# Output projection of a hybrid decoder step: the sample tile from unsplit float32 weights in two column groups, placed ahead of the last transposes

## The chip, the cores and the metric

The kernel runs on one core of one Trainium2 chip. Its engines work side by side and wait for each other on semaphores: TensorE (PE in the profile, PEld for its weight loads), VectorE (DVE), ScalarE (ACT), GpSimd (POOL) and SyncE (SP, which here only issues DMAs). The metric is the device time of one execution in microseconds (us); less is better. All times below come from runs on the chip.

## The reference

One inference step of a decoder layer for a prompt (16 meta tokens and 1024 tokens) and a sample group (8 sequences of 8 new tokens, so 64 rows). The part that the change touches is the very last one:

```python
y = jnp.concatenate([o_gla * jax.nn.silu(gg),
                     o_pool.astype(dt) * jax.nn.silu(pg),
                     o_fox.reshape(B, T, FOX_W).astype(dt) * jax.nn.silu(fg)], axis=-1) @ wo
return h + rmsnorm(y, post)          # wo is 1024 x 1024, h the input rows
```

Everything is float32. The attention part (`fox`) gives 384 of the 1024 columns of `y`, in three pairs of heads; its last pair of heads is what the kernel works on just before the projection.

## The kernel before, in words

Stages in order: input projection (up to about 470 us of the trace), softmax attention of the prompt in 12 "quarters" (pair of heads p = 0..2, 256 query rows q = 0..3) with the sample group's attention over its cached pages woven in, and from about 594 us the output projection.

**What sets the order.** The function `plan()` writes one list of steps; every engine walks it and does its own part of each step. The letters that matter here: `S` is a user of one of two score slots in PSUM (two banks each, taken in turn): a block of scores (`P1`), a block of transposes (`T`, with its quarter and number), or a tile of the output projection (`proj`). `V` is the product of a transposed block of probabilities with the values. `R sum` brings the inverse row sums to the rows of the quarter. `W k` copies row block k (of 8) of the output weights, rounded to the fast matmul format fp32r, into `woh` (ACT, `wo_high`); `X k` makes the remainder, raw weights minus `woh`, into `wol` (DVE, `wo_low`). `Y t` does the same split of the rows of `y`, `yh` on ACT (`y_high`) and `yl` on POOL. `E t` finishes a tile: sums of squares on ACT (`squares_out`), scaling, residual and output on DVE (`finish`). The table `TAIL` hangs `W`, `X` and `Y` steps behind units of the last two quarters.

**A tile of the projection** (`project_out`, `product`) is 3 products in fp32r for each of 8 row blocks and 2 halves of 512 columns: `yh` with `woh`, `yh` with `wol`, `yl` with `woh`; 48 matmuls of 512 columns. Nine tiles: first the sample's 64 rows, then eight of 128 prompt rows. The stationary operand is `y`, so the sample's 64 rows take as many matmuls of 512 columns as 128 rows do.

**Memory.** `wol_a` (remainders of row blocks 0 to 5) lies exactly over `wo_raw_a`, the raw weights, and `wol_b` (6 and 7) over `wo_raw_b`: `wo_low` writes each remainder in place. The tile's two halves lie in the two banks of its slot, on the same partitions; the slot is free for a next user when `finish` has read both halves (its second instruction on L1610).

A matmul of plain float32 is two instructions on TensorE in the trace (the products on L2053 and L2010); one of fp32r is one; a transpose is one.

Of the kernel before, what the change touches and what calls it, by code (L numbers as in the profile page):

```python
# [150 lines left out]
def plan():  # L151
# [66 lines left out]
    for n, t in enumerate(PROJ):  # L218
        if n >= 2:
            order.append(("Y", ("proj", t)))  # L220
        if n:
            order.append(("E", ("proj", PROJ[n - 1])))
        order.append(("S", ("proj", t)))
# [18 lines left out]
def slot_of(user):  # L242
    return SF[user] % 2


P1S = [k for k in SUSERS if k[0] == "P1"]
# [8 lines left out]
def build(nc, a, o):  # L255
    with ExitStack() as ctx:
# [6 lines left out]

        YF = sb("YF", [P, 14 * NT])
# [44 lines left out]
        def stage(*tensors):  # L309
            with ExitStack() as s:  # L310
                return [s.enter_context(nc.sbuf_tensor(n, d, t)) for n, d, t in tensors]

# [10 lines left out]
        wol_a, _, yh0, yl0, yh1, yl1, xres, zout, woh, wol_b, gpost = stage(  # L323
            ("wol_a", [P, 6, D], F32R), ("pad_a", [P, 6 * NT - 6 * D], F32),
            ("yh0", [P, KT, P], F32R), ("yl0", [P, KT, P], F32R), ("yh1", [P, KT, P], F32R),
# [103 lines left out]
        out_half, half_squared = sem("out_half"), sem("half_squared")  # L429

# [64 lines left out]
        def s_emptied(eng, user):  # L495
            eng.wait_ge(s_free[slot_of(user)], PROJ.index(user[1]) // 2 + 1)
# [276 lines left out]
        def _(pool):  # L773
# [114 lines left out]
            for n_, t in enumerate(PROJ):  # L888
                g.wait_ge(yhi_done, n_ + 1)
                m = P if t < NTILE else NS  # L890
                g.tensor_tensor(yl[n_ % 2][:, :, 0:m], Y[:, :, ycol(t):ycol(t) + m], yh[n_ % 2][:, :, 0:m].bitcast(F32),  # L891
                                ALU.subtract).then_inc(ylo_done, 1)

        @block.scalar
        def _(act):
# [236 lines left out]
            def squares_out(user):  # L1132

                t = user[1]
                n_ = PROJ.index(t)
                m = P if t < NTILE else NS
                low, high = slice(0, D // 2), slice(D // 2, D)
                act.wait_ge(out_half, n_ + 1)
                if n_:
                    act.wait_ge(d_y, 32 * n_)  # L1140
                act.activation(zout[0:m, low], s_slot(user)[0:m, low], ACT.Square, accum_out=zhalf[0:m, 0:1]  # L1141
                               ).then_inc(half_squared, 1)
# [3 lines left out]
                act.activation(zout[0:m, high], s_slot(user)[0:m, high], ACT.Square, accum_out=zstat[0:m, 0:1]  # L1146
                               ).then_inc(half_squared, 1)
# [13 lines left out]
            def y_high(n_):  # L1161

                t = PROJ[n_]
                m = P if t < NTILE else NS
                if t < NTILE:
                    drained(act, ("sum", 2, t // 2))
                else:
                    drained(act, ("s_outT", NB - 1))
                if n_ >= 2:
                    s_ready(act, ("proj", PROJ[n_ - 2]))  # L1170
                act.activation(yh[n_ % 2][:, :, 0:m], Y[:, :, ycol(t):ycol(t) + m], ACT.Copy).then_inc(yhi_done, 1)  # L1171

            for kind, key in PLAN:
                if kind == "Y":
                    y_high(PROJ.index(key[1]))
# [30 lines left out]
        def _(dve):  # L1206
# [389 lines left out]
            def wo_low(k):  # L1596
                dve.wait_ge(wohi_done, k + 1)
                dve.tensor_tensor(wol[k], wo_raw[k], woh[:, k, :].bitcast(F32), ALU.subtract).then_inc(wolo_done, 1)  # L1598

            def finish(user):  # L1600
# [7 lines left out]
                for n_half, cols in enumerate(halves):  # L1608
                    dve.wait_ge(half_squared, 2 * n_ + n_half + 1)
                    ins = dve.tensor_tensor(zout[0:m, cols], s_slot(user)[0:m, cols], gpost[0:m, cols], ALU.mult)  # L1610
# [73 lines left out]
        def _(pe):  # L1684
# [385 lines left out]
            def project_out(user):  # L2070
                t = user[1]
                n_ = PROJ.index(t)
                m = P if t < NTILE else NS
                s_taken(pe, user)
                out = s_slot(user)
                pe.wait_ge(yhi_done, n_ + 1)
                pe.wait_ge(ylo_done, n_ + 1)
                pe.wait_ge(wolo_done, KT)
                for half in range(2):
                    cols = slice(512 * half, 512 * half + 512)  # L2080
                    ins = product(out[0:m, cols], lambda k: (yh[n_ % 2][:, k, 0:m], yl[n_ % 2][:, k, 0:m]),
# [56 lines left out]
```

## Time and profile before

| | |
|---|---|
| Median of 3 runs | 701.57 us (701.45 to 702.39) |
| The profiled execution | 700.78 us |
| Its span in the trace | 699.1 us |
| PE busy | 658.0 us, 94% of the span |
| DVE, ACT, POOL busy | 393.3, 262.1, 142.9 us |
| Output projection, first matmul to the end | 593.82 to 699.1 us |

The trace starts later and ends earlier than the execution: 1.68 us lie around its span. Times in rows are counted from the start of the span. Busy times of one engine cannot be added to those of another, since they overlap; on PE an instruction's own duration holds its passage through the array, so that in a dense stream one starts before the one ahead of it has ended.

### The profile page before, as it was taken

Reading aid. Unit: us, or ns where it says so; the run is one execution under the profiler, and the core shown is the slowest. Engines: PE = TensorE matmul, PEld = TensorE weight load, DVE = VectorE, ACT = ScalarE, POOL = GpSimd, SP = SyncE. Lnnn points to the kernel's source line nnn. Section 1 sums busy time; section 2 is a strip of 40 time slices with the busy share of each in tenths; the row PEclk is TensorE's granted clock in tenths of the full one; section 3 lists DMA queues with packets and bytes.
Section 4 is the critical chain, followed back from the end, with each engine's and each line's share of the span. In section 5 each row is a group of like instructions: output and inputs, shape, how many; then the busy total and the mean of one; then the engine's idle time right before and its main releaser. Section 6 shows DMA issues by size and latency. Waiting matters only on the chain.

```text
span 699.1 us, 13106 instructions
## 1 busy us (share of the span) xinstructions
PE 658.0 (94%) x5120; PEld 565.0 (81%) x5120; DVE 393.3 (56%) x706; ACT 262.1 (37%) x480; POOL 142.9 (20%) x162
## 2 busy tenths in 40 slices
PE   2999999999999999999999989989999997999996
PEld 2799999898999889999999955766576655688885
DVE  4824926672455305169999965444433559345543
ACT  6637344111111346122121155645574566231321
POOL 4034112111111011233312040222222103112210
PEclk9999999999999999999999999999999999999999
DMA  8411103131100032352210381667676512033232
GB/s 248 124 38 49 43 1 75 29 94 31 32 26 8 4 84 97 98 166 77 61 31 1 119 272 42 179 180 209 186 226 176 207 37 100 9 98 106 75 122 90
DMA packets 60759, 67.29 MB, mean 96 GB/s; under 512 B 15188, under 2 KB 50907, under 8 KB 60697
## 3 DMA queue, kind: packets, MB, share of 16 engines
q1 hardware_dynamic: 55529, 51.37, 24.9%
q0 software_dynamic: 5168, 15.08, 7.3%
q8 instruction: 41, 0.67, 0.4%
q14 instruction: 21, 0.17, 0.1%
HBM read 57.71 MB, written 8.68 MB: 95 GB/s over the span
## 4 chain that ended last, share of the span: by engine, by line
PE 82%; DVE 9%; ACT 4%; issue 2%; SPq 1%; DMA 1%; DVEq 0%
PE PS L1764 14%; PE PS L1765 13%; PE PS L1766 13%; PE PS L1693 5%; PE PS L1692 5%; PE PS L1694 5%; PE PS L2053 3%; PE PS L2035 3%; PE PS L1988 3%; PE PS L2010 2%; PE PS L1953 2%; PE PS L1940 2%; DVE rows_odd L1576 2%; DVE YF L1455 1%; DVE wol_a L1598 1%
## 5 line engine op out<-in xcount | busy, mean ns | idle before, releaser
L1764 PE MATMUL PS<-xh,wh 128*128 128x368 f32 x576 | 196.1, 340 | 0.3 <-DVE RA L1392 0.3
L1765 PE MATMUL PS<-xl,wh 128*128 128x368 f32 x576 | 190.2, 330 | 0.0
L1766 PE MATMUL PS<-xh,wl 128*128 128x368 f32 x576 | 189.8, 329 | 0.0
L582 POOL TENSOR_TENSOR wl<-wr,wh 128x1024 fp32r<-128x1024 f32 x24 | 61.5, 2560 | 292.0 <-ACT wh L944 291.7
L1764 PEld LDWEIGHTS PS<-xh,wh 128*128 128x128 f32 x576 | 108.2, 188 | 4.4 <-issue 1.8
L1765 PEld LDWEIGHTS PS<-xl,wh 128*128 128x128 f32 x576 | 108.2, 188 | 0.9
L1766 PEld LDWEIGHTS PS<-xh,wl 128*128 128x128 f32 x576 | 108.2, 188 | 0.0
L1264 DVE TENSOR_TENSOR wr<-wr,small 128x1024 f32<-128x1024 f32 (+1 forms) x26 | 37.1, 1426 | 43.3 <-DMA wr<-in_w_in_dram 43.2
L1692 PE MATMUL PS<-woh,yh 128*128 128x512 f32 (+1 forms) x144 | 56.1, 390 | 0.6 <-DVE wol_b L1598 0.6
L1435 DVE RECIPROCAL RA<-RA 128x1104 f32<-128x1104 f32 x8 | 56.4, 7053 | 0.3
L1694 PE MATMUL PS<-woh,yl 128*128 128x512 f32 (+1 forms) x144 | 56.0, 389 | 0.0
L891 POOL TENSOR_TENSOR yl<-YF,yh 128x1024 fp32r<-128x1024 f32 (+1 forms) x9 | 22.7, 2520 | 107.3 <-ACT yh L1171 107.3
L2010 PE MATMUL PS<-YF 64*128 64x272 f32 (+9 forms) x168 | 34.7, 495 | 9.5 <-DVE pmax L1576 3.9
L1693 PE MATMUL PS<-wol_a,yh 128*128 128x512 f32 (+1 forms) x108 | 42.6, 395 | 0.0
L1610 DVE TENSOR_TENSOR zout<-PS,gpost 128x512 f32<-128x512 f32 (+1 forms) x18 | 12.4, 691 | 52.7 <-ACT zout L1141 31.2
L1190 ACT ACTIVATE kT<-PS 128x512 f32<-128x512 f32 x48 | 26.5, 594 | 37.3 <-PE PS L1940 37.3
L2053 PE MATMUL PS<-PT,VR 128*64 128x256 f32 (+1 forms) x288 | 33.8, 370 | 1.5 <-ACT PT L1184 0.9
L1069 ACT ACTIVATE RA<-PS 128x1104 f32<-128x1104 f32 x8 | 8.7, 1092 | 70.2 <-PE PS L1766 70.2
L1692 PEld LDWEIGHTS PS<-woh,yh 128*128 128x128 f32 (+1 forms) x144 | 26.1, 181 | 7.9 <-issue 0.8
L944 ACT ACTIVATE wh<-wr 128x1024 fp32r<-128x1024 f32 (+1 forms) x26 | 26.7, 1026 | 15.5 <-PE PS L1766 8.2
L2010 PEld LDWEIGHTS PS<-YF 64*128 64x128 f32 x168 | 12.7, 185 | 23.6 <-DVE pmax L1576 9.8
L1694 PEld LDWEIGHTS PS<-woh,yl 128*128 128x128 f32 (+1 forms) x144 | 26.2, 182 | 6.6
(305 smaller groups left out, 1084.2 us busy)
## 6 DMA issues: line engine op xcount, KB each, us to landing
wr<-in_w_in_dram SPq DMA_DIRECT2D x24, 512.0 KB, 3.7
kpage<-in_cache_fox_k_dram SPq DMA_DIRECT2D x64, 192.0 KB, 2.7
RA<-in_cache_fox_v_dram POOLq DMA_DIRECT2D x32, 192.0 KB, 3.7
pagesB<-in_cache_fox_v_dram POOLq DMA_DIRECT2D x32, 192.0 KB, 3.6
YF<-in_x_prompt_dram SPq DMA_DIRECT2D x8, 512.0 KB, 6.8
xres<-in_x_prompt_dram SPq DMA_DIRECT2D x8, 512.0 KB, 3.9
out_y_p_dram<-zout SPq DMA_DIRECT2D x16, 256.0 KB, 2.1
wo_raw_a<-in_w_out_dram SPq DMA_DIRECT2D x6, 512.0 KB, 4.8
```

The lines of the kernel that those rows point to most:

```text
L582: eng.tensor_tensor(low, wr[:, c % 2, :, 0:m], wh[:, c % 2, :, 0:m].bitcast(F32), ALU.subtract).then_inc(wlo_done, 1)
L944: act.activation(wh[:, c % 2, :, 0:m], wr[:, c % 2, :, 0:m], ACT.Copy).then_inc(whi_done, 1)
L1264: dve.tensor_tensor(w, w, gpre[:, :, None].to_broadcast([P, KT, m]), ALU.mult).then_inc(wg_done, 1)
L1435: link(dve.reciprocal(g, g))
L1692: pe.matmul(out, sh, mh, start=(k == 0), stop=False)
L1693: pe.matmul(out, sh, ml, start=False, stop=False)
L1694: ins = pe.matmul(out, sl, mh, start=False, stop=(k == KT - 1))
L1764: pe.matmul(out, high, xh[:, k, cols], start=(k == 0), stop=False)
L1765: pe.matmul(out, high, xl[:, k, cols], start=False, stop=False)
L1766: ins = pe.matmul(out, low, xh[:, k, cols], start=False, stop=(k == KT - 1))
L2010: ins = pe.matmul(s_head(user, i)[:, 0:c1 - c0], QK[rows, 3 + p, q0:q0 + P], QK[rows, p, c0:c1], start=True, stop=(d0 >= c1))
L2053: ins = pe.matmul(out[64 * i:64 * i + 64, P * tiles[0]:P * tiles[0] + m], VR[:, b, HD * h:HD * h + HD], pt[:, at:at + m], start=(s == 0 an ...
```

## The change

The sample tile of the output projection is no longer made from split operands. It multiplies the sample's 64 rows of `y` with the raw float32 weights: 8 row blocks, for each one matmul for the lower 512 columns and one for the upper. The lower half goes to partitions 0 to 63 of one bank, the upper to partitions 64 to 127 of the other (`out_part`), so the two matmuls of a pair use different column groups of the array. Its step `S` moves in the plan: it stood behind everything of the attention, and now follows the transposes (2,3,3), ahead of the last transposes (2,3,4); its `E` follows (2,3,4). It thereby takes the slot that the first prompt tile takes next.

Since the raw weights must stay readable, `wol_a` moves over the keys and queries (`QK`), which the last block of scores is the last to read, and `wo_low(0)` waits for that block. `wol_b` stays over `wo_raw_b`: the sample tile takes row blocks 6 and 7 first, and `wo_low(6)` waits for them (`sample_late`). The sample's `Y` step, its split on ACT and POOL, is gone. `X 0` to `X 3` and `X 6` move back in the plan.

```diff
-TAIL = {(2, 2, 0): [("W", 0), ("W", 1)], (2, 2, 1): [("X", 0), ("W", 2)],
-        (2, 2, 2): [("X", 1), ("X", 2), ("W", 3)], (2, 2, 3): [("X", 3), ("W", 4), ("Y", SAMPLE)],
+TAIL = {(2, 2, 0): [("W", 0), ("W", 1)], (2, 2, 1): [("W", 2)],
+        (2, 2, 2): [("X", 0), ("X", 1), ("W", 3)], (2, 2, 3): [("X", 2), ("X", 3), ("W", 4)],
...
-        (2, 3, 3): [("X", 6), ("W", 7)], (2, 3, 4): [("X", 7)]}
+        (2, 3, 3): [("W", 7), ("S", SAMPLE), ("X", 6), ("X", 7)], (2, 3, 4): [("E", SAMPLE)]}
...
+        _, wol_a = stage(("pad_y", [P, 8 * NT], F32), ("wol_a", [P, 6, D], F32R))
         YF = sb("YF", [P, 14 * NT])
...
+        def out_part(user, half):
+
+            r = slice(NS * half, NS * half + NS) if user[1] == NTILE else slice(0, P)
+            return s_head(user, half)[r, :]
...
             def wo_low(k):
+                if k == 0:
+                    s_ready(dve, P1S[-1])
+                elif k == 6:
+                    dve.wait_ge(sample_late, 1)
...
             def project_out(user):
                 t = user[1]
-                n_ = PROJ.index(t)
-                m = P if t < NTILE else NS
                 s_taken(pe, user)
+                if t == NTILE:
+                    drained(pe, ("s_outT", NB - 1))
+                    late_first = [6, 7, 0, 1, 2, 3, 4, 5]
+                    for k in late_first:
+                        pe.wait_ge(d_wo[k], 16)
+                        y = Y[:, k, ycol(t):ycol(t) + NS]
+                        lower = pe.matmul(out_part(user, 0), y, wo_raw[k][:, 0:D // 2], start=(k == 6),
+                                          stop=(k == 5), skip_group_check=True)
+                        upper = pe.matmul(out_part(user, 1), y, wo_raw[k][:, D // 2:D], start=(k == 6),
+                                          stop=(k == 5), skip_group_check=True)
+                        if k == 7:
+                            upper.then_inc(sample_late, 1)
+                    lower.then_inc(out_half, 1)
+                    upper.then_inc(s_full, 1)
+                    return
```

The order on TensorE at the end of the attention, before. `rows_odd` are the probabilities (transposes), `PT` and `VR` the transposed probabilities and values, `ebend` the inverse sums; the last row opens the sample tile:

```order
L2053 MATMUL PS<-PT,VR 64x256 [waits pt_dve]
L2053 MATMUL PS<-PT,VR 64x256 x3
L2035 MATMUL PS<-ident,rows_odd 128x128 [waits pt_act]
L2035 MATMUL PS<-ident,rows_odd 128x128
L2053 MATMUL PS<-PT,VR 64x256 [waits pt_act]
L2053 MATMUL PS<-PT,VR 64x256 x3
L2053 MATMUL PS<-PT,VR 64x256 [waits pt_dve]
L2053 MATMUL PS<-PT,VR 64x256 x3
L2053 MATMUL PS<-PT,VR 64x128 [waits pt_act]
L2053 MATMUL PS<-PT,VR 64x128
L2065 MATMUL PS<-ident,ebend 64x128 [waits inv_done,ring3_free1]
L1692 MATMUL PS<-woh,yh 64x512 [waits ylo_done,wolo_done,yhi_done,pt_dve]
```

The same place after (the lines are six or so further down), with the sample tile's 16 matmuls cut to the first two pairs and the last, and the first prompt tile at the end:

```order
L2059 MATMUL PS<-PT,VR 64x256 [waits pt_dve]
L2059 MATMUL PS<-PT,VR 64x256 x3
L2085 MATMUL PS<-wo_raw_b,YF 64x512 [waits d_wo6,ring3_free2,pt_act]
L2087 MATMUL PS<-wo_raw_b,YF 64x512
L2085 MATMUL PS<-wo_raw_b,YF 64x512 [waits d_wo7]
...
L2085 MATMUL PS<-wo_raw_a,YF 64x512 [waits d_wo5]
L2087 MATMUL PS<-wo_raw_a,YF 64x512
L2041 MATMUL PS<-ident,rows_odd 128x128 [waits pt_dve]
...
L2071 MATMUL PS<-ident,ebend 64x128 [waits inv_done,ring3_free1]
L2071 MATMUL PS<-ident,ebend 64x128 x3
L1698 MATMUL PS<-woh,yh 128x512 [waits ylo_done,wolo_done,yhi_done,s_free1]
```

The sample tile stands between the first values of the last quarter and its last transposes, and the first prompt tile now waits for `s_free1`, the emptying of the sample's slot.

The order on VectorE in the same stretch, before (`YF` by `PS` are the two multiplications that end a quarter):

```order
L1598 TENSOR_TENSOR wol_a<-wo_raw_a,woh 128x1024 [waits wohi_done] x3
L1638 TENSOR_TENSOR YF<-YF,PS 128x256 [waits pv_done]
L1645 TENSOR_TENSOR YF<-YF,PS 128x256 [waits o_free,ring_full]
L1594 RECIPROCAL ebend<-ebend 128x4 [waits ring_full,exp_done]
L1632 COPY PT<-PS 128x1024 [waits pv_done,s_full]
L1598 TENSOR_TENSOR wol_a<-wo_raw_a,woh 128x1024 [waits wohi_done] x2
L1632 COPY PT<-PS 128x1024 [waits pv_done,s_full]
L1598 TENSOR_TENSOR wol_b<-wo_raw_b,woh 128x1024 [waits wohi_done] x2
L1638 TENSOR_TENSOR YF<-YF,PS 128x256 [waits pv_done]
L1645 TENSOR_TENSOR YF<-YF,PS 128x256 [waits o_free,ring_full]
L1610 TENSOR_TENSOR zout<-PS,gpost 64x512 [waits half_squared,d_post]
```

And after:

```order
L1603 TENSOR_TENSOR wol_a<-wo_raw_a,woh 128x1024 [waits wohi_done,s_full]
L1603 TENSOR_TENSOR wol_a<-wo_raw_a,woh 128x1024 [waits wohi_done] x3
...
L1638 COPY PT<-PS 128x1024 [waits pv_done,s_full]
L1603 TENSOR_TENSOR wol_a<-wo_raw_a,woh 128x1024 [waits wohi_done] x2
L1638 COPY PT<-PS 128x1024 [waits pv_done,s_full]
L1603 TENSOR_TENSOR wol_b<-wo_raw_b,woh 128x1024 [waits wohi_done,sample_late]
L1603 TENSOR_TENSOR wol_b<-wo_raw_b,woh 128x1024 [waits wohi_done]
L1616 TENSOR_TENSOR zout<-PS,gpost 64x512 [waits half_squared,d_post]
L1616 TENSOR_TENSOR zout<-PS,gpost 64x512 [waits half_squared]
```

One more remainder (`X 0`) stands ahead of the copies, and the finishing of the sample tile now stands ahead of the last quarter's two multiplications, which follow it.

## Rows read from the trace of the kernel before

**Rows 1.** The page: busy time by engine, and the chain that ended last by engine.

```profile
PE 658.0 (94%) x5120; PEld 565.0 (81%) x5120; DVE 393.3 (56%) x706; ACT 262.1 (37%) x480; POOL 142.9 (20%) x162
PE 82%; DVE 9%; ACT 4%; issue 2%; SPq 1%; DMA 1%; DVEq 0%
```

**Rows 2.** The chain that ended last, 579 to 594: start us, us, what.

```profile
579.08 4.57 DVE wol_a L1598 x3
...
591.41 2.28 DVE wol_b L1598 x2
```

**Rows 3.** Timeline of PE: start, us, instructions, in brackets idle before and releaser.

```profile
582.50 5.08 PE L2035 MATMUL PS<-ident,rows_odd 128*16 128x128 f32 x28 [2.41 <-ACT rows_odd L1129]
587.51 1.95 PE L2053 MATMUL PS<-PT,VR 128*64 128x256 f32 x16
589.39 0.44 PE L2035 MATMUL PS<-ident,rows_odd 128*128 128x128 f32 x2
589.76 1.08 PE L2053 MATMUL PS<-PT,VR 128*64 128x256 f32 x8
591.46 1.30 PE L2053 MATMUL PS<-PT,VR 128*64 128x256 f32 x12 [0.62 <-DVE PT L1632]
592.60 0.66 PE L2065 MATMUL PS<-ident,ebend 128*64 128x128 f32 x8
593.82 0.41 PE L1692 MATMUL PS<-woh,yh 128*64 128x512 f32 x1 [0.57 <-DVE wol_b L1598]
...
604.93 0.39 PE L1692 MATMUL PS<-woh,yh 128*128 128x512 f32 x1
```

**Rows 4.** Groups by shape, 587.4 to 589.5 and 593.8 to 604.9: busy us, mean ns.

```profile
L2053 PE MATMUL PS<-PT,VR 128*64 128x256 f32 x16 | 1.9, 385 | 0.0
...
L1692 PE MATMUL PS<-woh,yh 128*64 128x512 f32 x16 | 6.3, 393 | 0.6 <-DVE wol_b L1598 0.6
```

**Rows 5.** Stretches: length, busy by engine (count), granted clock, DMA share, GB/s.

```profile
583.80:587.10 3.30, 3.19 (x16) 2.79 (x15) 3.20 (x6) 3.13 (x4) 0.97 (x1) 0.50 0.04 9
587.10:593.80 6.70, 5.53 (x50) 3.26 (x49) 6.70 (x5) 2.43 (x4) 2.09 (x1) 1.00 0.00 0
```

**Rows 6.** Timeline of ACT.

```profile
579.54 0.62 ACT L1171 ACTIVATE yh<-YF 128x512 fp32r<-128x512 f32 x1
...
583.14 1.03 ACT L1184 ACTIVATE PT<-PS 128x1024 f32<-128x1024 f32 x1 [0.69 <-PE PS L2035]
...
587.15 1.99 ACT L1159 ACTIVATE woh<-wo_raw_b 128x1024 fp32r<-128x1024 f32 x2
```

**Rows 7.** Timeline of DVE.

```profile
579.08 4.57 DVE L1598 TENSOR_TENSOR wol_a<-wo_raw_a,woh 128x1024 fp32r<-128x1024 f32 x3
...
584.63 1.20 DVE L1632 COPY PT<-PS 128x1024 f32<-128x1024 f32 x1
585.75 4.53 DVE L1598 TENSOR_TENSOR wol_a<-wo_raw_a,woh 128x1024 fp32r<-128x1024 f32 x2
...
591.33 2.34 DVE L1598 TENSOR_TENSOR wol_b<-wo_raw_b,woh 128x1024 fp32r<-128x1024 f32 x2
```

**Rows 8.** Timeline of POOL.

```profile
580.25 2.32 POOL L891 TENSOR_TENSOR yl<-YF,yh 128x512 fp32r<-128x512 f32 x1 [34.64 <-ACT yh L1171]
586.13 3.06 POOL L891 TENSOR_TENSOR yl<-YF,yh 128x1024 fp32r<-128x1024 f32 x1 [3.56 <-ACT yh L1171]
```

**Rows 9.** Timeline of ACT, then of DVE: finishing of the sample tile and the first prompt tile.

```profile
605.13 0.59 ACT L1146 ACTIVATE zout<-PS 64x512 f32<-64x512 f32 x1 [4.54 <-PE PS L1694]
...
614.72 0.60 ACT L1141 ACTIVATE zout<-PS 128x512 f32<-128x512 f32 x1 [6.04 <-DMA out_y_s_dram<-zout]
...
615.44 0.29 ACT L1144 ACTIVATE small<-small 128x1 f32<-128x1 f32 x1
616.18 0.60 ACT L1146 ACTIVATE zout<-PS 128x512 f32<-128x512 f32 x1 [0.44 <-PE PS L1694]
...
616.90 0.69 DVE L1610 TENSOR_TENSOR zout<-PS,gpost 128x512 f32<-128x512 f32 x1 [0.77 <-ACT zout L1146]
```

More of the change, by code:

```diff
@@ L216, in plan @@
     order += [("V", unit) for unit in behind] + [("R", ("sum",) + behind[0][:2])]
-    for n, t in enumerate(PROJ):
+    for n, t in enumerate(PROJ[1:], 1):
         if n >= 2:
-            order.append(("Y", ("proj", t)))
-        if n:
-            order.append(("E", ("proj", PROJ[n - 1])))
+            order += [("Y", ("proj", t)), ("E", ("proj", PROJ[n - 1]))]
         order.append(("S", ("proj", t)))
@@ L243, in slot_of @@
     return SF[user] % 2
+OUT_USERS = [k for k in SUSERS if k[0] == "proj"]
+OUT_OF_SLOT = {k: sum(slot_of(o) == slot_of(k) for o in OUT_USERS[:i + 1]) for i, k in enumerate(OUT_USERS)}
 P1S = [k for k in SUSERS if k[0] == "P1"]
@@ L261, in sem, with stage @@
             return ctx.enter_context(nc.semaphore(name))
+        def stage(*tensors):
+            with ExitStack() as s:
+                return [s.enter_context(nc.sbuf_tensor(n, d, t)) for n, d, t in tensors]
+        _, wol_a = stage(("pad_y", [P, 8 * NT], F32), ("wol_a", [P, 6, D], F32R))
         YF = sb("YF", [P, 14 * NT])
@@ L887, in _ @@
                     load_bias(2)
-            for n_, t in enumerate(PROJ):
+            for n_, t in enumerate(PROJ[1:]):
                 g.wait_ge(yhi_done, n_ + 1)
-                m = P if t < NTILE else NS
-                g.tensor_tensor(yl[n_ % 2][:, :, 0:m], Y[:, :, ycol(t):ycol(t) + m], yh[n_ % 2][:, :, 0:m].bitcast(F32),
+                g.tensor_tensor(yl[n_ % 2][:, :, :], Y[:, :, ycol(t):ycol(t) + P], yh[n_ % 2][:, :, :].bitcast(F32),
                                 ALU.subtract).then_inc(ylo_done, 1)
@@ L1140, in squares_out @@
                     act.wait_ge(d_y, 32 * n_)
-                act.activation(zout[0:m, low], s_slot(user)[0:m, low], ACT.Square, accum_out=zhalf[0:m, 0:1]
+                act.activation(zout[0:m, low], out_part(user, 0), ACT.Square, accum_out=zhalf[0:m, 0:1]
                                ).then_inc(half_squared, 1)
@@ L1145, in squares_out @@
                 s_ready(act, user)
-                act.activation(zout[0:m, high], s_slot(user)[0:m, high], ACT.Square, accum_out=zstat[0:m, 0:1]
+                act.activation(zout[0:m, high], out_part(user, 1), ACT.Square, accum_out=zstat[0:m, 0:1]
                                ).then_inc(half_squared, 1)
@@ L1161, in y_high @@
             def y_high(n_):
[L1163 to L1168, printed above, removed]
+                t = PROJ[1 + n_]
+                drained(act, ("sum", 2, t // 2))
                 if n_ >= 2:
-                    s_ready(act, ("proj", PROJ[n_ - 2]))
-                act.activation(yh[n_ % 2][:, :, 0:m], Y[:, :, ycol(t):ycol(t) + m], ACT.Copy).then_inc(yhi_done, 1)
+                    s_ready(act, ("proj", PROJ[n_ - 1]))
+                act.activation(yh[n_ % 2][:, :, :], Y[:, :, ycol(t):ycol(t) + P], ACT.Copy).then_inc(yhi_done, 1)
             for kind, key in PLAN:
                 if kind == "Y":
-                    y_high(PROJ.index(key[1]))
+                    y_high(PROJ.index(key[1]) - 1)
                 elif kind == "W":
@@ L1609, in finish @@
                     dve.wait_ge(half_squared, 2 * n_ + n_half + 1)
-                    ins = dve.tensor_tensor(zout[0:m, cols], s_slot(user)[0:m, cols], gpost[0:m, cols], ALU.mult)
+                    r = slice(NS, 2 * NS) if t == NTILE and n_half else slice(0, m)
+                    ins = dve.tensor_tensor(zout[0:m, cols], out_part(user, n_half), gpost[r, cols], ALU.mult)
                 ins.then_inc(s_free[slot_of(user)], 1)
@@ L2071, in project_out @@
                 t = user[1]
-                n_ = PROJ.index(t)
-                m = P if t < NTILE else NS
                 s_taken(pe, user)
+                if t == NTILE:
[13 more added lines that the diff above has]
+                    return
                 out = s_slot(user)
+                n_ = PROJ.index(t) - 1
                 pe.wait_ge(yhi_done, n_ + 1)
@@ L2080, in project_out @@
                     cols = slice(512 * half, 512 * half + 512)
-                    ins = product(out[0:m, cols], lambda k: (yh[n_ % 2][:, k, 0:m], yl[n_ % 2][:, k, 0:m]),
+                    ins = product(out[:, cols], lambda k: (yh[n_ % 2][:, k, :], yl[n_ % 2][:, k, :]),
                                   lambda k: (woh[:, k, cols], wol[k][:, cols]))
```

11 lines of the change are left out of this document (4 added, 7 removed).

## The prediction, made before the changed kernel ran

> **What bounds the kernel now.** I read the page first: PE is busy for 94% of the span and holds 82% of the chain that ended last [rows 1]. So a change that shortens PE's own work should show, unless something else ends the waits at that place. Then I followed the chain around the point where attention hands over to the projection. There it leaves PE: from 579.08 to 593.69 us it runs through VectorE's remainders of the weights and its copies, and returns to PE with the first matmul of the sample tile [rows 2]. The timeline of PE over the same stretch shows what that costs: idle for 2.41 us before 582.50 (for the exponentials of ACT), 0.62 us before 591.46 (for VectorE's copy of the transposes), 0.57 us before 593.82 (for the last remainder), and a sample tile that runs from 593.82 to 604.93, 11.11 us for 48 matmuls, 0.231 us each [rows 3]. From there PE is dense to the end, so whatever moves the start of the first prompt tile (604.93) moves the end of the kernel by as much: the 94.2 us from there to 699.1 stay as they are.
>
> The task is therefore to find when the first prompt tile can start after the change.
>
> **Where the new tile starts.** On PE it follows the values of units (2,3,0) and (2,3,1), which begin at 587.51 and make way at 589.39 [rows 3]. It waits for raw weights (ACT is reading the last two blocks from 587.15, so they have landed [rows 6]), for the sample's attention output (which VectorE applies ahead of its remainders of 579.08) and for the slot of (2,3,2), which ACT copies ahead of those last two blocks: all past. What stands ahead of 587.51 hardly moves. VectorE gets a fourth remainder in front of its copy of (2,3,1), some 1.15 us, but loses a companion: the sample's `yl` on POOL goes. In this trace the two engines take turns there: the three remainders of 579.08 take 4.57 us, where the undisturbed pair at 591.33 takes 2.34, 1.17 each [rows 7]. So three cost 1.06 us more than 3 x 1.17 = 3.51, while POOL works on its piece at 580.25 [rows 8]. Four undisturbed ones make 4 x 1.17 = 4.68, ending at 583.76 for 583.65: 0.1 us later. The copy at 584.63 keeps its time within that [rows 7]. ACT loses the sample's `yh` (it stood 0.52 us in front of the exponentials [rows 6]), so PE resumes at 582.0 for 582.50; but the transposes (2,3,3) wait for VectorE's copy at 584.63, so I count this gain as zero (bounds 0 and 0.5). Start of the tile: 589.4, between 588.9 and 589.6.
>
> **How long it takes.** No row shows float32 with 512 columns. The nearest is the product with the values: float32, 128 rows by 64 stationary columns, two column groups in turn, 256 columns. 16 instructions start within 589.39 - 587.51 = 1.88 us, 0.1175 us each [rows 3]. Do they really run in pairs? One of these instructions of 256 columns lasts 385 ns, about as long as one fp32r instruction of 512 columns (393 ns) [rows 4], which in a dense stream takes 0.231 us of the array. So it occupies its columns for about 0.231 us too, and a pace of 0.1175 is two at a time. The new tile has 8 x 2 matmuls, 32 instructions of 512 columns. Doubling the row's pace: 32 x 0.235 = 7.5 us. If the part of the pace that isn't streaming doesn't double, it is somewhat less, 7.2. If the two groups ran one after the other, 32 x 0.47 = 15.0 us. I take 7.5, since the shape and the pairing are those of the row; only the columns and the two banks differ.
>
> A rule speaks against full pairing, though the row shows a factor of two within some per cent [rows 3, 4]. The Trainium skill (TensorE: Matmul & The Clock Gate, Measured speedup vs the span model) reports 2.38x for three column groups at 512 columns, not three. Taken over as 2.38/3 = 79% of two, an estimate from that page, the tile would take about 9.4 us. The row's own shape decides for me; as a mechanism it is a rival below.
>
> **From the tile to the first prompt tile.** Two things follow 589.4 + 7.5 = 596.9.
>
> PE's own queue: transposes 0.37 us (589.39 to 589.76), values of (2,3,2) 1.0, of (2,3,3) and (2,3,4) 1.14 (591.46 to 592.60), inverse sums 0.66 [rows 3]: 3.2 us, to 600.1. The two waits of 0.62 and 0.57 us go, since the copy of (2,3,3) and the remainders of 591.33 [rows 7] run beside the new tile. The last two remainders now wait for its first two pairs: 589.4 + 8 x 0.235 = 591.3, when VectorE comes to them anyway; they end at 593.7, six us early.
>
> The slot: the prompt tile needs both halves of the sample read by VectorE. ACT first has a small copy of the last transposes (PE hands over at 597.2, it ends at 597.6), then squares of the lower half. On the first prompt tile: lower squares 614.72, small step at 615.44 (0.29 us, so the upper squares could start at 615.66), then 0.72 us from the upper squares to the second multiplication and 0.69 us for that [rows 9]. That is 0.94 + 0.72 + 0.69 = 2.35 us from the start of the lower squares: 597.6 + 2.35 = 600.0, plus about 0.1 us for PE to see it.
>
> Both ends meet at 600.1 (bounds: 599.3, if the queue ahead moves up and the tile takes 7.2; 607.6, if the groups run one after the other). What is queued behind `finish` on VectorE are the two multiplications of the last quarter, read only by the seventh and eighth prompt tiles: no cost. From the sample's upper squares (605.13) to the landed output for which the next lower squares waited (614.72) it is 9.6 us [rows 9]. Put at 598.5 it ends at 608.1, ahead of 611.2 when the first prompt tile is complete, so PE is not held there. The split of the second prompt tile has from 601 to 611.
>
> **The sum.** Sample tile 11.1 to 7.5: -3.6. Waits gone: -1.2. Slot wait and rounding: 0 to +0.1. Together -4.8 us (604.93 to 600.1), so 700.78 - 4.8 = 696.0 for an execution like the profiled one. That one lies 0.8 us under the median, 701.57; I take the difference from the median: 701.57 - 4.8 = 696.8 us.
>
> **Rivals.**
> - *The queue ahead moves up.* After its 2.41 us of idling PE runs at 1.2 GHz: granted clock 0.50 from 583.80 to 587.10, full after [rows 5], and the transposes of (2,3,2) and (2,3,3) fall into it. The new idle time is 0.5 us shorter. If the clock stays up, the 8 transposes of (2,3,3), which start near 585.9 and take 1.6 us to 587.51, take half as long: the tile starts up to 0.8 us earlier. For it: the shorter gap; against: 1.9 us idle may still be enough. Time 696.1.
> - *The slow stretch lands on the new tile.* The same clock drop, but later. The Trainium skill (TensorE: Matmul & The Clock Gate, What's actually happening) has the gate following recent activity and free-running against the kernel, so that its place may shift; no row here shows a second placing. 3.3 us at half speed [rows 5] cost 1.65 us: 698.4. Against: in this trace it is over by 587.1.
> - *Pairing is incomplete.* With 512 columns the pairs lose a quarter of what pairing saves in the row of 256: 7.5 + (15.0 - 7.5)/4 = 9.4 us for the tile, 1.9 us more: 698.7. For it: no row has 512 columns; against: longer streams should hide the weight loads better, not worse. (It is also what the page's 79% would make of it.)
> - *The slot wait ends last, by more*: ACT or VectorE reach the sample half a microsecond to one later than I count (the upper half lies on other partitions than its output, which no row shows). 697.5.
> - *Slower: the column groups don't overlap.* Two banks and 512 columns may behave unlike one bank and 256. Then the tile takes 15.0 us, ends at 604.4, and the prompt tile starts at 607.6: +2.7, 704.2. The kernel is slower from the point where the tile takes 7.5 + 4.8 = 12.3 us, a pairing of 1.2 or worse. The row with 0.1175 us a piece speaks against it.
>
> **How the numbers follow.** Forecast as summed, with the slot wait a few tenths off: 0.50. Queue moves up: 0.20. Later slot wait: 0.12. Slow stretch on the tile: 0.06. Incomplete pairing: 0.07. Groups in series: 0.05. The likeliest is 696.8. Eight in ten lie between 695.6 (the tile at 7.2 and the queue moved up by all of 0.8, together 1.1 us, and 0.1 for the median's own spread) and 698.5. What a measurement of this kernel tells from no change is about 0.2%, 1.4 us: slower only in the last case, 0.05; the two cases near 698.6 are still faster by 3 us; 0.93 faster, 0.02 the same.
>
> **What would show it.** In the changed kernel's timeline: 32 instructions of the new tile (lines L2085 and L2087) at 0.22 to 0.24 us each, from about 589.4 to 596.9; no idle time for the last remainder; the first prompt matmul near 600.1, released by VectorE's multiplication or by nothing; the span near 694.3. I am wrong if the new instructions come at over 0.3 us, if the prompt tile waits over 0.5 us for its slot, or if the granted clock is 0.5 anywhere after 588.

## The result, and the profile after

The changed kernel takes 697.0 us (median of 4 runs, 696.53 to 697.7), the kernel before 701.98 us beside it (4 runs, 701.45 to 703.63): ratio 0.9922, 95% interval 0.9905 to 0.9938. Its profiled execution took 697.7 us with a span of 696.1. Repeated with the experiments it took 696.68 against 701.58: 0.9929 [0.9916, 0.9942].

The page after, against [rows 1]: PE is busy 4 us less and the share of VectorE in the chain that ended last falls from 9% to 8%.

```profile
PE 654.0 (94%) x5104; PEld 560.0 (80%) x5104; DVE 392.2 (56%) x706; ACT 261.3 (38%) x479; POOL 139.9 (20%) x161
PE 80%; DVE 8%; ACT 4%; issue 3%; SPq 3%; DMA 1%; DVEq 0%; ACTq 0%
```

The timeline of PE at the hand-over (start, us, instructions, in brackets idle before and releaser), against [rows 3]:

```profile
583.72 1.48 PE L2041 MATMUL PS<-ident,rows_odd 128*16 128x128 f32 x12 [1.90 <-ACT rows_odd L1134]
585.44 1.09 PE L2041 MATMUL PS<-ident,rows_odd 128*128 128x128 f32 x8 [0.24 <-ACT PT L1185]
587.69 1.09 PE L2041 MATMUL PS<-ident,rows_odd 128*128 128x128 f32 x8 [1.16 <-DVE PT L1638]
588.71 1.95 PE L2059 MATMUL PS<-PT,VR 128*64 128x256 f32 x16
590.49 0.59 PE L2085 MATMUL PS<-wo_raw_b,YF 128*64 128x512 f32 x1
590.50 0.59 PE L2087 MATMUL PS<-wo_raw_b,YF 128*64 128x512 f32 x1
590.92 0.59 PE L2085 MATMUL PS<-wo_raw_b,YF 128*64 128x512 f32 x1
...
597.46 0.44 PE L2041 MATMUL PS<-ident,rows_odd 128*128 128x128 f32 x2
597.83 2.17 PE L2059 MATMUL PS<-PT,VR 128*64 128x256 f32 x20
599.82 0.66 PE L2071 MATMUL PS<-ident,ebend 128*64 128x128 f32 x8
600.69 0.50 PE L1698 MATMUL PS<-woh,yh 128*128 128x512 f32 x1 [0.21 <-DVE zout L1616]
```

The new tile is 16 pairs: the two instructions of a pair start within 0.01 us of each other and the next pair 0.43 us later. From 590.49 to 597.46 it takes 6.97 us, where the old tile took 11.11. The two waits that stood at 591.46 and 593.82 are gone; 0.21 us of waiting for the slot has come, ahead of the first prompt tile at 600.69.

The timeline of VectorE, against [rows 7]:

```profile
580.43 0.36 DVE L1685 TENSOR_TENSOR YF<-YF,PS 64x24 f32<-64x24 f32 x2
580.82 4.63 DVE L1603 TENSOR_TENSOR wol_a<-wo_raw_a,woh 128x1024 fp32r<-128x1024 f32 x4
...
586.44 1.19 DVE L1638 COPY PT<-PS 128x1024 f32<-128x1024 f32 x1
587.55 4.40 DVE L1603 TENSOR_TENSOR wol_a<-wo_raw_a,woh 128x1024 fp32r<-128x1024 f32 x2
...
593.01 2.34 DVE L1603 TENSOR_TENSOR wol_b<-wo_raw_b,woh 128x1024 fp32r<-128x1024 f32 x2
...
599.94 0.69 DVE L1616 TENSOR_TENSOR zout<-PS,gpost 64x512 f32<-64x512 f32 x1 [0.27 <-ACT zout L1151]
```

The prediction let two ends meet at the first prompt tile: PE's own queue, and the sample's finishing through ACT and VectorE. The chain that ended last shows that the finishing was the later one, by the 0.21 us above.

```profile
597.52 0.39 PE PS L2041 x2
597.93 0.38 ACT PT L1185
598.32 0.58 ACT zout L1146 x2
598.91 0.29 ACT small L1149
599.22 0.69 ACT zout L1151 x2
599.94 0.70 DVE zout L1616
600.69 0.50 PE PS L1698
```

**One clock for all runs.** The profiled executions reach this place at different times: the step that both kernels share, VectorE's application of the sample's attention output (64x24, which I call A), stands at 578.70 in the kernel before, at 582.16 in a second execution of it, at 580.43 in the changed one. Short stretches of a lower granted clock earlier in the program differ from one execution to the next: in the second execution of the kernel before the clock is 0.50 from about 242 to 249 us, in the first it is full from the start to 583. No run here shows what sets them. So a difference of single spans says nothing about this change to within 3.5 us. The row of the kernel before:

```profile
578.70 0.36 DVE L1679 TENSOR_TENSOR YF<-YF,PS 64x24 f32<-64x24 f32 x2
```

I split each span at two rows: A, and P, the first matmul of the first prompt tile (L1692 before, L1698 after). All times in us; "half" is the mean time from one half of a prompt tile (24 matmuls) to the next, over the later tiles.

| kernel | A | P | span | A to P | P to end | A to end | half |
|---|---|---|---|---|---|---|---|
| before | 578.70 | 604.93 | 699.1 | 26.23 | 94.17 | 120.40 | 5.48 |
| before, again (r_before) | 582.16 | 608.39 | 702.6 | 26.23 | 94.21 | 120.44 | 5.48 |
| changed | 580.43 | 600.69 | 696.1 | 20.26 | 95.41 | 115.67 | 5.55 |
| changed, again (r_after) | 581.33 | 601.58 | 696.9 | 20.25 | 95.32 | 115.57 | 5.55 |
| e1_old_place | 582.07 | 603.35 | 698.7 | 21.28 | 95.35 | 116.63 | 5.55 |
| e2_one_group | 579.11 | 606.09 | 701.5 | 26.98 | 95.41 | 122.39 | 5.55 |
| e3_moved | 580.00 | 606.89 | 702.1 | 26.89 | 95.21 | 122.10 | 5.55 |
| e4_longer_gap | 580.28 | 600.54 | 695.9 | 20.26 | 95.36 | 115.62 | 5.55 |
| e5_shift_32 | 579.60 | 599.86 | 695.4 | 20.26 | 95.54 | 115.80 | 5.57 |
| e6_shift_1920 | 580.50 | 600.75 | 696.4 | 20.25 | 95.65 | 115.90 | 5.57 |
| v1_early_inplace | 579.82 | 596.57 | 690.8 | 16.75 | 94.23 | 110.98 | 5.48 |
| v2_early_moved | 578.63 | 595.38 | 690.7 | 16.75 | 95.32 | 112.07 | 5.55 |

Two executions of one kernel agree within 0.02 us from A to P and within 0.1 from P to the end. So these columns tell tenths apart, where medians have intervals of about 1 us. They show that the sum of the prediction came out (A to end: 4.7 us less, where 4.8 was forecast) though two of its parts did not: up to P the change gains 5.97 us, and from P on it gives 1.2 back.

The two kernels themselves ran again with the experiments.

> The changed kernel once more, for its own spread. In its first trace the sample tile took 6.97 us from the first of its matmuls to the next instruction, the first prompt tile started 0.2 us after PE had finished its queue, and the eight prompt tiles ran at 5.55 us a half instead of 5.48. If the slower pace of the prompt tiles belongs to the kernel (where the remainders lie, or what the column groups leave behind), it is 5.55 again; if it belongs to the execution, it may be 5.48 here, and the end then comes 1.2 us earlier against the start of the first prompt tile. Ratio to the kernel before: 0.992 to 0.994.

> The kernel before once more, for what of its first trace belongs to it. In that trace the prompt tiles ran at 5.48 us a half after the first half of the first one, and PE's granted clock was 0.50 from 583.8 to 587.1, behind an idle time of 2.41 us. If both belong to the kernel, the pace is 5.48 again and a stretch at 0.50 stands again some 4 us behind the start of that idle time; if the pace belongs to the execution, it may be 5.55 here. Ratio 1.000.

Measured: the changed kernel 696.68 us as above; the kernel before 703.33, 1.0008 [0.9993, 1.0024] of itself. The pace of the prompt tiles belongs to the kernel and not to the execution: 5.55 us again in the one, 5.48 in the other. The stretch at half clock also came back in the kernel before, about 5 us behind A as the first time (587.1 to 590.5, for 583.7 to 587.1).

### The profile page after: what moved, and what is told of

Read it like the earlier page. It is cut to its first block, busy times and chain, and to the rows that moved or that the text cites. A ratio compares the mean times of both kernels' runs of the same rounds, so it can differ in the third digit from the quotient of the medians.

```text
span 696.1 us, 13072 instructions
## 1 busy us (share of the span) xinstructions
PE 654.0 (94%) x5104; PEld 560.0 (80%) x5104; DVE 392.2 (56%) x706; ACT 261.3 (38%) x479; POOL 139.9 (20%) x161
## 4 chain that ended last, share of the span: by engine, by line
PE 80%; DVE 8%; ACT 4%; issue 3%; SPq 3%; DMA 1%; DVEq 0%; ACTq 0%
PE PS L1770 13%; PE PS L1771 13%; PE PS L1772 13%; PE PS L1698 4%; PE PS L1699 4%; PE PS L1700 4%; PE PS L2059 3%; PE PS L2041 3%; PE PS L1994 3%; PE PS L2016 2%; PE PS L1959 2%; PE PS L1946 2%; DVE rows_odd L1577 2%; DMA wr<-in_w_in_dram 1%; DVE YF L1456 1%
## 5 line engine op out<-in xcount | busy, mean ns | idle before, releaser
L1698 PE MATMUL PS<-woh,yh 128*128 128x512 f32 x128 | 50.5, 395 | 0.2 <-DVE zout L1616 0.2
L1700 PE MATMUL PS<-woh,yl 128*128 128x512 f32 x128 | 50.2, 392 | 0.0
L896 POOL TENSOR_TENSOR yl<-YF,yh 128x1024 fp32r<-128x1024 f32 x8 | 19.8, 2475 | 105.1 <-ACT yh L1172 105.1
L1699 PE MATMUL PS<-wol_a,yh 128*128 128x512 f32 x96 | 38.0, 396 | 0.0
L1638 DVE COPY PT<-PS 128x1024 f32<-128x1024 f32 (+1 forms) x18 | 17.2, 956 | 23.9 <-PE PS L2059 12.2
L860 POOL DMA_DIRECT2D RA<-in_cache_fox_v_dram x32 | 17.4, 545 | 57.8 <-issue 57.8
```

The costliest lines, as they stand in the source:

```text
L1698: pe.matmul(out, sh, mh, start=(k == 0), stop=False)
L1699: pe.matmul(out, sh, ml, start=False, stop=False)
L1700: ins = pe.matmul(out, sl, mh, start=False, stop=(k == KT - 1))
```

## Experiments

**e1: the new tile in the old place** (behind the last values, as the old one).

```diff
+    order += [("S", SAMPLE), ("E", SAMPLE)]
...
-        (2, 3, 3): [("W", 7), ("S", SAMPLE), ("X", 6), ("X", 7)], (2, 3, 4): [("E", SAMPLE)]}
+        (2, 3, 3): [("W", 7), ("X", 6), ("X", 7)]}
```

> The sample tile as in the changed kernel (raw float32 weights, two column groups), but at its old place behind all of the attention, with its finishing right behind it. Theory (the gain is the shorter tile and that no remainder is waited for; the place itself gives little): attention ends as before, 5.8 us after the values of unit (2,3,0) begin, with the 0.62 us wait for VectorE's copy kept; the tile follows at once and takes 7.0 us; the first prompt tile follows it at once, since its slot is another. From the values of (2,3,0) to the first prompt tile 12.7 us, for 12.0 in the changed kernel (1.9 + 7.0 + 3.1 and a slot wait of 0.2) and 17.4 before. So 0.5 to 0.8 us slower than the changed kernel, about 4.2 us faster than before. Rival (the place is what matters, because VectorE's last remainders stay on the path): the prompt tile waits for the last remainder, 14 us or more, some 2 us slower than the changed kernel.

Measured: 698.52 us, 0.9958 [0.9944, 0.9973] of before. A to P is 21.28 us, 1.02 more than in the changed kernel (0.5 to 0.8 was expected) and 4.95 less than before. The medians lie further apart, 1.8 us, but A itself came late in the profiled execution and others of this run are scattered over 3.6 us; I go by the rows. Timeline of PE, then of VectorE:

```profile
590.34 1.95 PE L2060 MATMUL PS<-PT,VR 128*64 128x256 f32 x16
...
594.77 1.30 PE L2060 MATMUL PS<-PT,VR 128*64 128x256 f32 x12 [1.10 <-DVE PT L1639]
595.90 0.66 PE L2072 MATMUL PS<-ident,ebend 128*64 128x128 f32 x8
596.34 0.59 PE L2086 MATMUL PS<-wo_raw_b,YF 128*64 128x512 f32 x1
```

```profile
593.50 1.21 DVE L1639 COPY PT<-PS 128x1024 f32<-128x1024 f32 x1
598.31 2.36 DVE L1604 TENSOR_TENSOR wol_b<-wo_raw_b,woh 128x1024 fp32r<-128x1024 f32 x2 [3.60 <-PE PS L2088]
```

The wait for VectorE's copy stays, and is 1.10 us, not 0.62: the queue ahead of it on PE ends earlier, the copy does not. That is the place's worth, about 1 us. The other 4.95 us come with the tile in its old place: 4.10 are its own shorter run (596.34 to 603.35), 0.54 the queue from A to the values of (2,3,0), which the full clock shortens (below; its cause is open), and 0.31 the rest. In that rest the wait for the remainder is gone (0.57 us [rows 3]) and the wait for the copy is 0.48 longer. The rival, that VectorE's last remainders stay on the path, is refuted: they run from 598.31, beside the tile, and the prompt tile doesn't wait for them.

**e2: the same tile, both halves in one column group** (the same 64 rows, so nothing can run in pairs).

```diff
-            r = slice(NS * half, NS * half + NS) if user[1] == NTILE else slice(0, P)
+            r = slice(0, NS) if user[1] == NTILE else slice(0, P)
...
-                    r = slice(NS, 2 * NS) if t == NTILE and n_half else slice(0, m)
+                    r = slice(0, m)
```

> As the changed kernel, but both halves of the sample tile on partitions 0 to 63, so in one column group, each in its own bank. Theory (the two groups overlap fully): the 32 instructions, which started in pairs every 0.429 us, now start one by one every 0.43 us; the tile takes 13.8 us for 7.0, and the kernel is 6.8 us slower than the changed one, about 2 us slower than the kernel before. Rival (the gain came from leaving out the split and the third product, not from pairing): the tile takes 7 to 9 us here as well and the time is that of the changed kernel.

Measured: 704.51 us, 1.0045 [1.0031, 1.0060] of before: slower than it. Timeline of PE:

```profile
589.16 1.02 PE L2085 MATMUL PS<-wo_raw_b,YF 128*64 128x512 f32 x2
590.02 1.02 PE L2087 MATMUL PS<-wo_raw_b,YF 128*64 128x512 f32 x2
...
602.04 1.02 PE L2087 MATMUL PS<-wo_raw_a,YF 128*64 128x512 f32 x2
602.99 0.44 PE L2041 MATMUL PS<-ident,rows_odd 128*128 128x128 f32 x2
```

Two instructions take 0.86 us from one row to the next, 0.43 each, and the tile 602.99 - 589.16 = 13.83 us. Against 6.97 that is a factor of 1.98: the column groups run beside each other almost fully, with 512 columns and two banks. A to P is 6.7 us longer than in the changed kernel. Without the pairing the change would have lost: from A to the end it takes 2.0 us more than the kernel before.

**e3: the remainders moved, the sample tile as before.** The kernel before with the changed kernel's address and order of the first four remainders:

```diff
+        _, wol_a = stage(("pad_y", [P, 8 * NT], F32), ("wol_a", [P, 6, D], F32R))
...
-        wol_a, _, yh0, yl0, yh1, yl1, xres, zout, woh, wol_b, gpost = stage(
-            ("wol_a", [P, 6, D], F32R), ("pad_a", [P, 6 * NT - 6 * D], F32),
+        _, yh0, yl0, yh1, yl1, xres, zout, woh, wol_b, gpost = stage(
+            ("pad_a", [P, 6 * NT], F32),
...
+                if k == 0:
+                    s_ready(dve, P1S[-1])
```

> The kernel before with one part of the change: the remainders of row blocks 0 to 5 lie over keys and queries instead of over the raw weights, and remainders 0 to 3 stand where the change puts them; the sample tile is made from split operands at its old place, its split on ACT and POOL stays. Two questions. Pace: if the place of the remainders in memory makes the prompt tiles slower, they run at 5.55 us a half here; if the column groups or the execution do, at 5.48. Queue ahead: four remainders now stand ahead of VectorE's copy of (2,3,1) while POOL still makes its piece; if the two engines take turns, they take 4 x 1.15 + 1.1 = 5.7 us for 4.57 and everything behind starts 1.1 us later. Time: 1.1 us slower than before with the old pace, 2.4 us slower with the new one.

Measured: 704.78 us, 1.0049 [1.0031, 1.0066] of before; from A to the end 1.70 us more, for the 2.4 that was expected. Timeline of VectorE, of POOL and of PE:

```profile
580.38 5.70 DVE L1600 TENSOR_TENSOR wol_a<-wo_raw_a,woh 128x1024 fp32r<-128x1024 f32 x4
...
587.07 1.19 DVE L1634 COPY PT<-PS 128x1024 f32<-128x1024 f32 x1
```

```profile
581.54 2.33 POOL L891 TENSOR_TENSOR yl<-YF,yh 128x512 fp32r<-128x512 f32 x1 [34.62 <-ACT yh L1171]
```

```profile
588.32 1.67 PE L2037 MATMUL PS<-ident,rows_odd 128*128 128x128 f32 x8 [1.71 <-DVE PT L1634]
589.91 3.00 PE L2055 MATMUL PS<-PT,VR 128*64 128x256 f32 x16
```

The move alone costs twice. Before P it costs 0.66 us: four remainders beside the sample's `yl` take 5.70 us, and the copy comes 1.1 us later after A than before (7.07 against 5.93). PE waits 1.71 us for it; the stretch at half clock comes behind this second wait (granted clock 0.50 from 588.7 to 592.1) and falls on the values. After P it costs 1.04 us, with a half at 5.55. So the slower pace of the prompt tiles comes without the new tile, from the moved remainders or their new order; v1 and v2 below separate the two.

**e4: the gap of 1.90 us made as long as before.** An extra copy of the sample on ACT, read by nobody, in front of the exponentials:

```diff
-        (2, 2, 2): [("X", 0), ("X", 1), ("W", 3)], (2, 2, 3): [("X", 2), ("X", 3), ("W", 4)],
+        (2, 2, 2): [("X", 0), ("X", 1), ("W", 3)], (2, 2, 3): [("X", 2), ("X", 3), ("W", 4), ("Q", 0)],
...
+                if kind == "Q":
+                    drained(act, ("s_outT", NB - 1))
+                    act.activation(yh1[:, :, 0:NS], Y[:, :, ycol(NTILE):ycol(NTILE) + NS], ACT.Copy)
```

> As the changed kernel, but ACT again makes a copy of the sample's 64 rows (which nothing reads) in front of the last exponentials, as the kernel before did; POOL makes none. So PE idles for 2.4 us again instead of 1.9 before the second half of the transposes (2,3,0), and everything else is as in the changed kernel. Theory (the shorter idle time is what keeps PE's clock up; with 1.9 us none of 4 traces had a slow stretch there, with 2.4 us both had one): a stretch at 0.50 of 3 us or so comes back near there, and costs 0.6 us if it lies on the transposes of (2,3,3), up to 1.6 us if it lies on the sample tile. Rival (the slow stretch falls where it likes): the clock stays at 1.0 there and the time is that of the changed kernel, since VectorE's copy of (2,3,1), not the exponentials, sets when the transposes (2,3,3) can start.

Measured: 697.24 us, 0.9932 [0.9916, 0.9948]; A to P 20.26, as in the changed kernel. Timeline of PE:

```profile
584.09 1.48 PE L2044 MATMUL PS<-ident,rows_odd 128*16 128x128 f32 x12 [2.42 <-ACT rows_odd L1134]
...
587.54 1.09 PE L2044 MATMUL PS<-ident,rows_odd 128*128 128x128 f32 x8 [0.63 <-DVE PT L1641]
```

The gap is 2.42 us and no slow stretch follows. Stretches of e4, then one of the second execution of the kernel before (length, busy by engine, granted clock third from the end):

```profile
585.00:586.00 1.00, 0.76 (x8) 0.52 (x7) 0.86 (x3) 1.00 (x2) 0.00 (x0) 1.00 0.42 82
588.00:589.00 1.00, 1.00 (x10) 0.73 (x10) 1.00 (x2) 1.00 (x2) 1.00 (x1) 1.00 0.00 0
```

```profile
588.00:589.00 1.00, 1.00 (x6) 1.00 (x5) 1.00 (x3) 1.00 (x2) 0.00 (x0) 0.50 0.00 0
```

My theory that the shorter gap keeps the clock up isn't borne out: here the clock stays up with the long gap. This is one execution, so that the slow stretch merely falls elsewhere by chance isn't excluded. The 0.5 us of gap are also worth nothing: the wait for VectorE's copy shrinks by as much (1.16 to 0.63), as the prediction argued.

**e5 and e6: the remainders shifted**, by 32 bytes in each partition and by 1920 (from 51840 to 51872 and 53760; before they lie at 103392):

```diff
-        _, wol_a = stage(("pad_y", [P, 8 * NT], F32), ("wol_a", [P, 6, D], F32R))
+        _, wol_a = stage(("pad_y", [P, 8 * NT + 8], F32), ("wol_a", [P, 6, D], F32R))
```

> As the changed kernel, but the remainders of row blocks 0 to 5 lie 32 bytes further on in each partition (51872 for 51840). All other operands of the projection, and the remainders of the kernel before, start at 32 beyond a multiple of 64 bytes; those of the changed kernel start at a multiple of 64. Theory (the alignment of the moving operand against 64 bytes sets PE's pace): the prompt tiles run at 5.48 us a half again, 1.1 to 1.2 us less from the first prompt tile to the end, and the kernel is 1.2 us faster than the changed one. Rival (it is the region, or the distance to the other operands): 5.55 us a half and the same time as the changed kernel.

> As the changed kernel, but the remainders of row blocks 0 to 5 lie 1920 bytes further on in each partition (53760, again a multiple of 64). Theory of alignment: 5.55 us a half, as in the changed kernel. Rival (the distance between the remainders and the other operands decides, not the alignment): the pace differs from 5.55.

Measured: 697.17 us, 0.9937 [0.9921, 0.9953], and 697.90, 0.9946 [0.9929, 0.9963]; a half takes 5.57 us in both. Neither brings 5.48 back, so alignment against 64 bytes is not the cause (51872 shares it with 103392, 51840 and 53760 don't). Nor is the pace exactly that of 51840: it is 0.02 us a half slower at both, and no run explains this.

**v1 and v2: the tile in the idle time.** PE idles for the exponentials while the sample's attention output is there, and the raw weights land in time for a pair every 0.43 us. The tile therefore goes in front of the first transposes of the last quarter, into a bank of the ring that is free there (lower half of the columns on rows 0 to 63, upper half on 64 to 127). In v1 the remainders also go back over `wo_raw_a`, each written when the tile has read its block; v2 keeps them where the change put them. Six remainders and the split of the first prompt tile's activations are ordered earlier in both, ahead of the copy of (2,3,1).

```diff
+STILE = ("sample_tile",)
+PLAN.insert(PLAN.index(("S", ("T", 2, 3, 0))), ("R", STILE))
...
+            if user == SAMPLE:
+                return bank(STILE)[NS * half:NS * half + NS, :]
...
-                if k == 0:
-                    s_ready(dve, P1S[-1])
-                elif k == 6:
-                    dve.wait_ge(sample_late, 1)
+                if k < 7:
+                    dve.wait_ge(sample_late, k + 1)
+                else:
+                    ring_ready(dve, STILE)
```

> The sample tile as in the changed kernel, but into one PSUM bank of another ring (lower half on partitions 0 to 63, upper on 64 to 127), and placed ahead of the first transposes of the last quarter (2,3,0), where PE idles for 1.9 us and then waits 1.2 us more for VectorE. The remainders lie over the raw weights again, each made as soon as the sample tile has read its row block; the first prompt tile's split stands earlier. From the start of the transposes (2,3,0) in the changed kernel (19.5 us ahead of its first prompt tile) the same work without idle time is 7.0 (tile) + 4.0 (32 transposes) + 1.9 + 0.4 + 2.0 + 0.6 = 15.9 us, with one or two waits of 0.3 for copies 16.5; so the first prompt tile starts 3.0 us earlier. Theory (the pace of the prompt tiles depends on where the remainders lie, not on the column groups that ran before): 5.48 us a half, 1.2 us less to the end. Together 4.2 us faster than the changed kernel, about 9 us (1.3%) faster than before. Rival (the column-group tile leaves PE at the slower pace): 5.55 us a half, 3.0 us faster than the changed kernel. Rival (VectorE, with six remainders behind the tile's reads, becomes the bound): a wait of over 1 us for its copy of (2,3,1), gain of 2 us or less.

> As v1, but with the remainders of row blocks 0 to 5 over keys and queries, as in the changed kernel, so that VectorE can start them 1 us earlier. Theory: the same start of the first prompt tile as in v1 within 0.3 us, and 5.55 us a half, so 1.2 us slower than v1 and 3.0 us faster than the changed kernel. Rival (the pace has nothing to do with the place): the same pace and time as v1.

Measured: v1 692.78 us, 0.9873 [0.9853, 0.9893] of before (702.64 beside it); v2 693.06, 0.9877 [0.9860, 0.9893]. Timeline of PE in v1:

```profile
586.95 0.59 PE L2092 MATMUL PS<-wo_raw_b,YF 128*64 128x512 f32 x1
587.47 1.92 PE L2049 MATMUL PS<-ident,rows_odd 128*16 128x128 f32 x16
589.63 2.17 PE L2049 MATMUL PS<-ident,rows_odd 128*128 128x128 f32 x16 [0.24 <-ACT PT L1189]
...
595.97 0.66 PE L2079 MATMUL PS<-ident,ebend 128*64 128x128 f32 x8
596.57 0.49 PE L1706 MATMUL PS<-woh,yh 128*128 128x512 f32 x1
```

The gaps of 1.90 and 1.16 us and the slot's 0.21 are gone; A to P is 16.75 us, 3.5 less than in the changed kernel (3.0 was expected). Both halves of the tile in one bank still run in pairs. From P on, when all remainders are made in both, the two differ by address alone: 94.23 us in v1, 95.32 in v2. Both beat the two kernels of this case, v1 the kernel before by 9.9 us; between v1 and v2 the medians (0.3 us apart) decide nothing, only the profiled executions do.

## Why the prediction was right, and where it was wrong

**The tile: 7.5 forecast, 6.97 measured.** The mechanism was right, and shown by e2. The size was off: I doubled the pace of the row with 256 columns (0.1175 to 0.235 us an instruction), and the 512-column pairs come every 0.429 us, 0.215 an instruction. One group alone takes 0.43 us (e2), not the 0.47 I used. The bound of 7.2 lay too high as well: a pair takes 0.235 us with 256 columns and 0.429 with 512, so by these two some 0.04 us of it doesn't grow with the columns (an estimate; no run shows what it is). The rival of incomplete pairing is refuted by the factor of 1.98. The Trainium skill (TensorE: Matmul & The Clock Gate, Measured speedup vs the span model) reports 2.38x for three column groups. Its loss doesn't carry over to two groups of float32 here, and neither do the 9.4 us.

**The waits: 1.2 us forecast to go, less 0 to 0.1 for the slot; 1.3 went.** Without queue and tile, the way from A to P shrinks from 6.31 us to 5.01, the slot's 0.21 included. From the tile's end to P it is 597.46 to 600.69, 3.23 us, for the 3.2 of the forecast: the queue itself took 0.2 less, the slot wait 0.2 more. So the rival of a later slot wait came in small, by 0.21 us where it had put half a microsecond or more.

**The queue ahead of the tile: 0 forecast, 0.5 us gained.** From the first transposes of (2,3,0) to the values of (2,3,0) it was 579.48 to 587.51 and 582.95 to 590.93 before (8.03 and 7.98 us), and 581.22 to 588.71 and 582.12 to 589.60 after (7.49 and 7.48). This is the rival "the queue moves up", and its size lies within its bounds. Its condition came true, the clock does not fall; its reason, the shorter gap, isn't what e4 shows. In the three executions with the old sample tile (before, r_before, e3) a stretch at half clock comes behind the gap, in e3 only 4.9 us behind it, after a further wait of 1.71; in none of the nine with the new tile (in v1 and v2 it fills the gap; the other seven idle there for 1.9 to 2.4 us). With VectorE's copy in the same place after A (6.01 us against 5.93), the full clock saves the half microsecond. Why the clock falls in the one form and not in the other, and whether the form has anything to do with it, stays open.

**The remainders ahead of the copy: 4.68 us forecast, 4.63 measured.** That VectorE and GpSimd take turns was read rightly from [rows 7, 8], and e3 shows the other side: with the sample's `yl` kept, the four take 5.70. The Trainium skill (SBUF — State Buffer, SBUF: two separate sides) describes a port pair that VectorE and GpSimd share as an exclusive lock, held for a whole instruction. The trace agrees: of e3's four remainders one, beside `yl`, lasts 2.29 us, the one behind it 1.21.

**The step that failed: "the 94.2 us from there to 699.1 stay as they are".** They became 95.4. A half of 24 matmuls takes 5.55 us for 5.48, some 3 ns more for each of them. The mean durations have hardly grown on the matmuls that read the moved remainder (395 to 396 ns); they have grown on those with `woh`, which hasn't moved (389 to 394 with `yh`). Groups by shape on PE, 620 to 680, before, changed, and v1:

```profile
L1692 PE MATMUL PS<-woh,yh 128*128 128x512 f32 x88 | 34.2, 389 | 0.0
L1693 PE MATMUL PS<-wol_a,yh 128*128 128x512 f32 x67 | 26.5, 395 | 0.0
```

```profile
L1698 PE MATMUL PS<-woh,yh 128*128 128x512 f32 x87 | 34.3, 394 | 0.0
L1699 PE MATMUL PS<-wol_a,yh 128*128 128x512 f32 x65 | 25.7, 396 | 0.0
L1700 PE MATMUL PS<-woh,yl 128*128 128x512 f32 x87 | 34.1, 392 | 0.0
```

```profile
L1706 PE MATMUL PS<-woh,yh 128*128 128x512 f32 x88 | 34.2, 389 | 0.0
```

With 0.07 us a half, the 16 halves cost 1.1 of the 1.2 us. I had priced the changed address of `wol_a` at nothing without naming it. e3 gives the slower pace to the old tile, v1 the faster one to the new, and v2 differs from v1 from P on by the address alone: where the remainders lie sets the pace, shown in both directions. By what mechanism is open: 51840, 51872 and 53760 are slow, 103392 is fast, and no other address was tried. (The kernel before itself runs the first three halves of its projection, the sample tile's two among them, at 5.56 and then at 5.48; no run explains that either.)

**The sum** of 4.8 us was met (4.73 from A to the end, 4.98 by the medians) because errors cancel: 1.2 us more gained up to P (0.5 tile, 0.5 queue, 0.1 to 0.2 waits), 1.2 us lost after it. That the total fits this closely is luck. The rivals "slow stretch on the tile" and "groups don't overlap" are refuted by the clock of 1.00 there and by the pairs. None of the three marks by which I would have called myself wrong appeared while PE worked (a new instruction takes 0.215 us, the slot wait 0.21, the clock is full from 588 to the last matmul at 689.40; from 692 on, with PE done, it is 0.50). None of them looked at the pace behind P, where the failed step lay. The span forecast for the profiled execution, 694.3, was missed (696.1), 1.7 us of it because A came that much later.

The last thing that the prediction named, the output of the sample ahead of the next finishing, came as worked out: ACT's lower squares of the first prompt tile start at 608.77, for 608.1, and PE isn't held.

```profile
608.77 0.60 ACT L1146 ACTIVATE zout<-PS 128x512 f32<-128x512 f32 x1 [6.00 <-DMA out_y_s_dram<-zout]
```

## What to carry to other kernels

For a tile of 64 rows it is worth trying to split its output columns over two column groups: here that halved it (13.83 to 6.97 us), and even with float32's dearer instructions it beat three split-precision products and freed the tile from the remainders of the weights. Not tried: the three fp32r products themselves in two column groups. If they paired as well, 24 pairs of 0.231 us would make about 5.5 us, an estimate; no run shows whether they do. Work that depends only on what is already there belongs in a gap of the bounding engine, not behind it: v1, with the address put back as well, gained twice what the change did. When a tensor is moved in memory, compare the pace of the dense stream that reads it, from a row that all versions share to the end, and don't rest on a sum that comes out: two errors of 1.2 us hid in this one.

## What the hardware showed that I had not expected

- Two column groups ran 1.98 times as fast as one: 16 pairs in 6.97 us against 32 single instructions in 13.83 (float32, 128 rows by 64 stationary columns, 512 moving columns), with the outputs in two banks and, by v1, also in one.
- The pace of dense matmuls depends on the address of one of their moving operands, and what grows is the time of those on other operands: 5.48 us for 24 with it at 103392 bytes, 5.55 at 51840, 5.57 at 51872 and 53760.
- A gap of 2.4 us on PE was followed by 3.4 us at half clock in three of three executions of kernels with the old tile (583.7 to 587.1 in the first; in e3 after a second wait), and not in the one execution with the new tile and the same gap.
